# Seven sums of squares on TensorE: two matmuls of the weights' form in place of one in full f32

## The reference: what is computed

```python
def rmsnorm(x, g):
    y = xf * lax.rsqrt(jnp.mean(xf * xf, axis=-1, keepdims=True) + EPS)
    return (y * g)

x = x + 0.5 * swiglu(rmsnorm(x, ffn1_norm[l]), ffn1_w_gu[l], ffn1_w_down[l])
x = x + token_mixing(rmsnorm(x, mix_norm[l]), w_in[l], lower_bounds[l], hg_norm[l], conv_w[l], conv_norm[l], w_out[l])
x = x + cross_attention(rmsnorm(x, xa_norm[l]), rmsnorm(mem, mem_norm[l]), xa_wq[l], xa_wkv[l], xa_wo[l])
x = x + 0.5 * swiglu(rmsnorm(x, ffn2_norm[l]), ffn2_w_gu[l], ffn2_w_down[l])
return rmsnorm(x, final_norm)
```

## Time and profile before

| | us |
|---|---|
| median of three executions | 1124.89 (1123.07 to 1125.19) |
| the profiled execution | 1124.98 |
| its span, first to last instruction | 1122.8 |
| PE busy | 1112.7 (99%) |
| DVE busy | 621.9 (55%) |
| ACT busy | 519.8 (46%) |
| POOL busy | 434.2 (39%) |

### The profile page before, as it was taken

How to read it: one execution, slowest core, us unless ns; L and a number is a source line. 1 busy time by engine, 2 the same in 40 slices (tenths; PEclk the granted TensorE clock), 3 DMA queues, 4 the chain that set the end, 5 groups by cost and what they waited for, 6 DMA issues and landing times.

```text
span 1122.8 us, 17338 instructions
## 1 busy us (share of the span) xinstructions
PE 1112.7 (99%) x6390; PEld 979.2 (87%) x6390; DVE 621.9 (55%) x907; ACT 519.8 (46%) x721; POOL 434.2 (39%) x544
## 2 busy tenths in 40 slices
PE   9999999999999999999999999999999999999997
PEld 7889999988888888888888888888899999988886
DVE  6887777452222668787568133463787777440012
ACT  6545555443323555654366443354455555552221
POOL 0000000486665534434448883173010000485551
PEclk9999999999999999999999999999999999999999
DMA  7276776323333221222313452123186675332312
GB/s 238 76 212 183 195 187 178 113 94 113 107 99 106 81 76 57 75 76 68 110 68 119 163 169 76 38 80 108 43 232 181 172 196 168 114 108 99 113 57 75
DMA packets 48626, 135.30 MB, mean 120 GB/s; under 512 B 4672, under 2 KB 10944, under 8 KB 48448
## 3 DMA queue, kind: packets, MB, share of 16 engines
q1 hardware_dynamic: 43344, 118.35, 31.2%
q0 software_dynamic: 4032, 14.68, 8.0%
q10 hardware_dynamic: 1200, 1.57, 0.4%
HBM read 132.49 MB, written 2.10 MB: 120 GB/s over the span
## 4 chain that ended last, share of the span: by engine, by line
PE 53%; POOL 24%; issue 21%; DVE 0%; DMA 0%; POOLq 0%; ACT 0%; DVEq 0%; SPq 0%
POOL wl L436 24%; PE bank L1411 9%; PE bank L1412 9%; PE bank L1413 9%; PE bank L1515 4%; PE bank L1514 4%; PE bank L1513 4%; PE score L1515 3%; PE score L1514 3%; PE score L1513 3%; PE o_bank L1515 1%; PE o_bank L1514 1%; PE o_bank L1513 1%; PE bank L1470 1%; PE bank L1474 1%
## 5 line engine op out<-in xcount | busy, mean ns | idle before, releaser
L436 POOL TENSOR_TENSOR wl<-raw,wh 128x256 fp32r<-128x256 f32 x512 | 409.6, 833 | 329.0 <-ACT wh L470 285.5
L470 ACT ACTIVATE wh<-raw 128x1024 fp32r<-128x1024 f32 x124 | 130.0, 1054 | 165.7 <-PE bank L1413 163.4
L1411 PE MATMUL bank<-xh,wh 128*128 128x512 f32 x488 | 194.7, 399 | 0.0
L1413 PE MATMUL bank<-xh,wl 128*128 128x512 f32 x488 | 190.2, 390 | 0.0
L1412 PE MATMUL bank<-xl,wh 128*128 128x512 f32 x488 | 190.1, 390 | 0.0
L450 POOL DMA_DIRECT2D raw<-w_all x28 | 24.3, 869 | 334.5 <-DMA raw<-w_all 334.5
L1411 PE MATMUL bank<-zr,wh 128*128 128x512 f32 (+1 forms) x374 | 141.0, 377 | 0.0
L1413 PE MATMUL bank<-zr,wl 128*128 128x512 f32 (+1 forms) x374 | 140.8, 377 | 0.0
L1412 PE MATMUL bank<-zr,wh 128*128 128x512 f32 (+1 forms) x374 | 140.8, 377 | 0.0
L900 DVE SCALAR_TENSOR_TENSOR x<-bank,x 128x512 f32<-128x512 f32 (+1 forms) x31 | 21.3, 686 | 173.3 <-PE bank L1413 173.3
L1411 PEld LDWEIGHTS bank<-xh,wh 128*128 128x128 f32 x488 | 91.7, 188 | 20.2 <-issue 1.4
(11 more groups left out here) (307 smaller groups left out, 2505.2 us busy)
## 6 DMA issues: line engine op xcount, KB each, us to landing
raw<-w_all SPq DMA_DIRECT2D x200, 512.0 KB, 3.3
raw<-w_all POOLq DMA_DIRECT2D x28, 512.0 KB, 5.4
zf<-w_all SPq DMA_DIRECT2D x28, 256.0 KB, 4.4
x<-x_t SPq DMA_DIRECT2D x8, 256.0 KB, 6.2
out_t<-x SPq DMA_DIRECT2D x8, 256.0 KB, 2.4
raw<-w_all SPq DMA_DIRECT2D x6, 256.0 KB, 6.1
memf<-mem_t ACTq DMA_DIRECT2D x1, 1024.0 KB, 7.0
raw<-w_all ACTq DMA_DIRECT2D x2, 256.0 KB, 4.3
```

The lines of the kernel that those rows point to most:

```text
L436: ins = nc.gpsimd.tensor_tensor(wl[:, slot, two], raw[:, slot, two], wh[:, slot, two].bitcast(f32), SUB)
L470: nc.scalar.activation(wh[:, slot, :], raw[:, slot, :], ACT.Copy).then_inc(hi_ready, 1)
L1411: nc.tensor.matmul(out_, a[0], b_[0], start=first, stop=False)
L1413: return nc.tensor.matmul(out_, a[1], b_[0], start=False, stop=last)
```

## The change

`sum_squares` for `mix`, `xa` and `ffn2`, and the N step of the four heads, no longer multiply the f32 sum by f32 `ones`. ScalarE copies the f32 data to an fp32r high part, VectorE subtracts it to give an fp32r low part, and TensorE multiplies both by a copy of the ones of type fp32r (`ones_r`), into the same bank. The sums of `ffn1`, `conv`, the memory and the last norm stay as they were. The new tiles lie on the memory of old ones (`sqr` on `sq`, `osq_l` on `osq`, `osq_h` on `onrm`). In the diff, the parts with `act` are ScalarE's program, those with `dve` VectorE's and those with `pe` TensorE's.

```diff
+            def acc_split(name):
+                act.wait_ge(sq_added, {"mix": Q_X1, "xa": Q_X2, "ffn2": Q_X3}[name] + KC)
+                nc.scalar.activation(sqr[:, 0, :], acc[:, :], ACT.Copy).then_inc(acc_hi, 1)
+
             def inverse_root(name, dst, src, width):
 
+                if name in ("mix", "ffn2"):
+                    acc_split(name)
                 if name not in ("ffn1", "mixcol"):
                     act.preload_act_table_set("natural_log_exp_and_others")
                 act.wait_ge(n_done, N[name] + 1)
...
                 if kind == "O":
                     act.wait_ge(o_done, h + 1)
                     nc.scalar.activation(osq[:, :], o_bank[:, :], ACT.Square).then_inc(osq_ready, 1)
+                    act.wait_ge(osq_ready, h + 1)
+                    if h > 0:
+                        act.wait_ge(cat_lo, h)
+                    nc.scalar.activation(osq_h[:, :], osq[:, :], ACT.Copy).then_inc(osq_hi, 1)
...
+            acc_split("xa")
             for g in range(KC):
                 ahead(U_KT + g)
...
+            dve.wait_ge(consts_ready, 1)
+            V_.tensor_copy(ones_r[:, :], ones[:, :]).then_inc(ones_ready, 1)
...
+            def acc_low(name):
+                dve.wait_ge(acc_hi, SPLIT[name] + 1)
+                V_.tensor_tensor(sqr[:, 1, :], acc[:, :], sqr[:, 0, :].bitcast(f32), SUB).then_inc(acc_lo, 1)
+
             def norm_of(name):
 
+                if name in ("mix", "ffn2"):
+                    acc_low(name)
                 dve.wait_ge(rms_ready, R[name] + 1)
...
                 if kind == "N":
 
+                    dve.wait_ge(osq_hi, h + 1)
+                    V_.tensor_tensor(osq_l[:, :], osq[:, :], osq_h[:, :].bitcast(f32), SUB).then_inc(osq_lo, 1)
                     dve.wait_ge(rms_ready, R["N", h] + 1)
...
+            acc_low("xa")
             for g in range(KC):
                 dve.wait_ge(kv_hi, g + 1)
...
             def sum_squares(name, added):
 
+                if name in SPLIT:
+                    pe.wait_ge(acc_lo, SPLIT[name] + 1)
+                    n_wait(name)
+                    pe.wait_ge(ones_ready, 1)
+                    nc.tensor.matmul(n_bank[:, :], ones_r[:, :], sqr[:, 0, :], start=True, stop=False)
+                    nc.tensor.matmul(n_bank[:, :], ones_r[:, :], sqr[:, 1, :], start=False, stop=True).then_inc(n_done, 1)
+                    return
                 pe.wait_ge(sq_added, added)
...
                 if kind == "N":
-                    pe.wait_ge(osq_ready, h + 1)
+                    pe.wait_ge(osq_lo, h + 1)
                     n_wait(("N", h))
-                    nc.tensor.matmul(n_bank[:, :], ones[:, :], osq[:, :], start=True, stop=True).then_inc(n_done, 1)
+                    pe.wait_ge(ones_ready, 1)
+                    nc.tensor.matmul(n_bank[:, :], ones_r[:, :], osq_h[:, :], start=True, stop=False)
+                    nc.tensor.matmul(n_bank[:, :], ones_r[:, :], osq_l[:, :], start=False, stop=True).then_inc(n_done, 1)
```

More of the change, by code:

```diff
@@ L125, in block_kernel @@
         acc = sb("acc", [128, T])
-        sq = sb("sq", [128, 2, T])
+        sq_mem = ExitStack()
+        sq = sb("sq", [128, 2, T], f32, sq_mem)
+        sq_mem.close()
+        sqr = sb("sqr", [128, 2, T], f32r)
         gbuf = sb("gbuf", [128, 2, T])
@@ L131, in block_kernel @@
         ones = sb("ones", [128, 128])
+        ones_r = sb("ones_r", [128, 128], f32r)
         ident = sb("ident", [128, 128])
@@ L180, in block_kernel @@
         S = sb("S", [128, NCH - 1, 128], f32, mix_mem)
-        osq = sb("osq", [128, T], f32, mix_mem)
-        onrm = sb("onrm", [128, T], f32, mix_mem)[:, :]
+        o_mem = ExitStack()
+        osq = sb("osq", [128, T], f32, o_mem)
+        onrm = sb("onrm", [128, T], f32, o_mem)[:, :]
+        o_mem.close()
+        osq_l = sb("osq_l", [128, T], f32r, mix_mem)
+        osq_h = sb("osq_h", [128, T], f32r, mix_mem)
         convC = sb("convC", [128, T], f32, mix_mem)
@@ L291, in block_kernel @@
         xn_new = sem("xn_new")
+        acc_hi = sem("acc_hi")
+        acc_lo = sem("acc_lo")
+        osq_hi = sem("osq_hi")
+        osq_lo = sem("osq_lo")
+        ones_ready = sem("ones_ready")
         xn_hi = sem("xn_hi")
@@ L366, in block_kernel @@
         N = {n: i for i, n in enumerate(n_uses)}
+        SPLIT = {"mix": 0, "xa": 1, "ffn2": 2}
         roots = [n for n in n_uses if isinstance(n, str) or n[0] == "N"]
```

## The result

The changed kernel takes 1153.87 us (median of 4 runs, 1150.48 to 1155.25) against 1123.99 us for the kernel before on the same chip (median of 4, 1123.07 to 1125.19). The ratio is 1.0262 (95% interval 1.0248 to 1.0276): slower, by 30 us. The profiled execution is the fastest of the four, 1150.48 us with a span of 1148.7.

A forecast was written before the change was run, and what follows sets the result against it. The prediction took PE (TensorE) as the bound nearly everywhere, busy 1112.7 of 1122.8 us. Waits of 24.7 us, less 2.8 saved, plus 5.1 for clock falls, made 27.0 on 1124.98: 1152 us, range 1143 to 1159.

The forecast's parts named there:

- The waits: At all seven changed sums, PE waits for late operands or, at xa, a weight unit: 24.7 us added in all.
- The rival of faster VectorE operations: In the heads' slots, slow VectorE operations turn fast: 6.6 us less, 1140 or 1145 us; chance 0.06.
- The xa term: Behind xa's sum, ScalarE's copy delays a weight unit through POOL, so PE waits 1.2 to 1.6 us, taken as 1.3.
- The saving: At each of seven sums, two fp32r matmuls occupy PE 0.40 us less than the f32 one: 2.8 us in all.
- The rival that the form saves nothing: At the seven sums, two fp32r matmuls occupy as much as the old sum: 2.8 us added; no separate chance.
- PE goes round the waiting sum: At the seven sums, PE runs the next group's matmuls meanwhile: 1122 us; chance 0.04, shared with other causes of no loss.
- The clock: PE's clock falls in the waits of heads 0, 1 and 2, costing 1.7 us each: 5.1 us in all.
- The program's start: PE's first eight matmuls run at double time, 3.54 us, losing 1.7; the forecast counts from an execution of 1124.98 us.

The follow-up runs named there:

- e1: The changed kernel with only the four head norms split, and mix, xa and ffn2 back in f32: 1148.58 us, ratio 1.0218 to the kernel before.
- e2: The changed kernel with only mix, xa and ffn2 split, and the heads back in f32: 1130.74 us, ratio 1.0053 to the kernel before.
- e6: The changed kernel with only the sum of xa split, as in the change: one profiled execution, span 1123.9 us.
- e8: The changed kernel with only mix split and VectorE's low part ahead of its memsets: one profiled execution, step of 1.40 us at the sum, less 0.40 behind it.
- e5: As e1, but TensorE multiplies only the high part in one f32 matmul, still waiting for the unused low part: 1150.78 us, ratio 1.0241 to the kernel before.
- e4: As e3, with xa and ffn2 also split, ScalarE's copies (and xa's low part) placed elsewhere, mix in f32: 1122.65 us, ratio 0.9983 to the kernel before.
- e3: As e1, but VectorE makes each head's low part one slot before TensorE's sum: 1121.85 us, ratio 0.9984 to the kernel before.
- e9: As e1, but TensorE takes each head's sum one weight group later, behind the next slot's group: 1133.18 us, ratio 1.0085 to the kernel before.

## Why the prediction was right

- *The waits.* 24.7 us predicted, 24.1 in the ledger, every place within 0.2. e1, e2, e6 and e8 show the places in groups or alone, and e5 that at the heads they are waits and nothing of the matmul's form. The rival of faster VectorE operations fell: in slot 15 they took 0.95 us again.
- *The xa term*, by way of ScalarE and POOL to a weight unit: 1.3 predicted, 1.29 in the ledger with the saving put in at 0.39. e6 shows that it isn't the sum's own operand, and in e4, with the copy at another place, the wait is gone.
- *The saving.* 0.40 a place, 2.8 in all; measured 0.28 and 0.32 behind the waits of head 3 and ffn2, 0.39 to 0.45 where PE didn't wait (e3 and e4). The rival that the form saves nothing fell with e3.
- *PE goes round the waiting sum*: no. In none of the six waits at a sum does a matmul of the following group start before it (the timeline of head 1 shows one of them), and all 6390 matmuls keep the order that they have in the kernel before.
- *The clock*, the step that was mis-sized and partly wrong. I had 5.1 us from three falls of 1.7, and expected none behind the four shorter waits. Three falls behind the long waits took 1.37, 1.93 and 2.39, together 5.7 us. But the clock also fell behind mix's wait of 1.9 us, for 1.6 us more, and in e2 behind that of ffn2 too. I had taken the stretch at the program's end for the shortest that brings a fall, and it wasn't.
- *The program's start.* I took the double durations there as given, and counted from an execution of 1124.98 us, of the upper group, where the median of before on the same chip is 1123.99. In the profiled execution of the change they lasted 1.8 us less long, which hid most of the extra clock loss in that run. The three other runs of the change have a mean granted clock of 0.985 against 0.989: over 1150 us that is by estimate 9 us more at half clock, 4.6 us of time, and they took 2.7 to 4.8 us longer. What exactly was longer in them isn't shown, as they have no trace.

The forecast of 1152 lies between the profiled execution (1150.5) and the median (1153.9). It is right by its waits. That the clock's 5.1 us come so near the net 5.5 of the ledger is luck: the fall behind mix and the larger falls behind the heads, 2.2 us that it lacked, met a start that came out 1.8 us short.

## What to carry to other kernels

Before an operand of a matmul gets a further step on another engine, look at where that engine stands when TensorE arrives, and not at how long the step takes: 0.7 us of VectorE work cost a wait of 6.2 us behind one slot's work, and none at that sum a slot earlier. A step in front of a producer's other work counts as well, as with the copy that held up a weight unit. And where TensorE is the bound, a wait costs itself and often a stretch at half clock behind it.

## What the runs showed of the hardware

- A full f32 matmul of 512 columns occupies TensorE for 0.86 us and an fp32r one for 0.23, so a sum in two fp32r parts saves 0.40 us; the ledger of e3 has 0.44 or 0.45 at each of four sums.
- The granted clock fell to the level of 1.2 GHz (rows of 0.51 to 0.64 over stretches of 4 to 6 us) behind PE's waits for the sum of heads 0, 1 and 2 in the change, e1 and e5 (4.8 us and more), behind the wait of 2.9 us for X in e9, behind mix's of 1.9 us in the change and e2, and behind ffn2's of 1.9 us in e2. It stayed at 2.4 GHz behind ffn2's of 1.9 us in the change, behind the 2.5 us for the convolution's sum in e9, and behind the waits of 1.0 to 1.6 us (head 3 in the change, e1 and e5; xa in the change, e2 and e6; mix in e8). The same wait had it fall in one kernel and not in the other, so its length alone doesn't decide; what does stays open. At head 1 the low clock is there when PE goes on, behind mix's wait in e2 it came 0.8 us later. Each fall took 1.4 to 2.7 us of time.
- At the program's start the clock rises between 4.4 and 10.4 us, differently from run to run, and until then PE works at the double time. Between the profiled executions of before (9.7) and of the change (4.9) that alone is 1.8 us, and it goes with the two groups of times: the profiled execution of e3 (10.4) lies in its upper group, that of e4 (4.8) in its lower one. For executions without a trace it isn't shown. The timeline of the change's first products, against the earlier trace rows:

```profile
5.78 1.17 PE L1513 MATMUL bank<-xh,wh 128*128 128x512 f32 x4 [0.93 <-ACT xh L715]
...
7.84 1.08 PE L1521 MATMUL bank<-xh,wl 128*128 128x512 f32 x4
```

Eight matmuls took 2.06 us here and 3.54 there.
